# A gated convolution and four pools on one Trainium2 core: spread of 1/rms one group earlier, a PSUM bank for each pool product, evacuations moved up

## Reference, cut to what matters

```python
x = rms_norm(h, norm_final)                  # end of the first block
...
xn = rms_norm_2(h, norm_mix[layer])
proj = einsum('bsd,de->bse', xn, w_in_even)  # 1024 x 2048
a_b, a_c, a_v, z_b = four slices of 512 of proj
y_a = a_b * causal_dwconv3(a_c * a_v, conv_a)
# multiscale_pool: 4 groups of 128 channels, windows 2, 4, 8, 16
outs.append((csg - shifted) / count - z32[:, :, g])
mixed = einsum('bsgc,gcd->bsgd', pooled, w_pool) * pool_scale
h = h + einsum('bse,ed->bsd', concatenate([y_a, y_b]), w_out_even)
```

## Time and profile before

| | us |
|---|---|
| median of three runs | 1690.48 |
| profiled execution, its own time | 1688.79 |
| its span | 1687.6 |
| TensorE busy in the span | 1608.8 |
| VectorE busy | 906.3 |
| ScalarE busy | 680.5 |
| GpSimd busy | 81.7 |
| `even` and `oe`, from 1110.29 to 1207.02 of the span | 96.73 |

### The profile page before, as it was taken

One profiled execution on the slowest core, in us unless ns is written; L12 is line 12 of the kernel. 1 busy time (PEld: TensorE's weight loads), 2 busy tenths in 40 slices (PEclk: granted clock), 3 DMA queues, 4 the chain that ended last, 5 costly groups with the idle time before them and its releaser, 6 DMA issues.

```text
span 1687.6 us, 25828 instructions
## 1 busy us (share of the span) xinstructions
PE 1608.8 (95%) x11251; PEld 1412.5 (84%) x11251; DVE 906.3 (54%) x1199; ACT 680.5 (40%) x917; POOL 81.7 (5%) x124
## 2 busy tenths in 40 slices
PE   5899999989999999989898999987999999999998
PEld 3678866767777778878668999987999999899998
DVE  4522277463243333356766555547677755477763
ACT  2411266342221221235564444433455445354452
POOL 4000043000000000000000000005000000000000
PEclk7799999999999999999898999998999999899999
DMA  9754542335554542243103555545455464455552
GB/s 254 236 195 151 175 36 23 119 107 200 174 185 165 174 150 94 81 149 124 53 2 103 197 176 170 183 156 172 150 176 185 160 205 150 135 181 184 178 178 70
DMA packets 242977, 251.27 MB, mean 149 GB/s; under 512 B 4797, under 2 KB 240672, under 8 KB 242864
## 3 DMA queue, kind: packets, MB, share of 16 engines
q1 hardware_dynamic: 240112, 244.34, 44.5%
q0 software_dynamic: 2464, 5.09, 2.6%
q10 hardware_dynamic: 288, 0.19, 0.0%
HBM read 248.55 MB, written 1.05 MB: 148 GB/s over the span
## 4 chain that ended last, share of the span: by engine, by line
PE 91%; DVE 4%; DMA 2%; ACT 1%; issue 1%; SPq 0%; DVEq 0%; ACTq 0%
PE psum L318 88%; PE psum L732 2%; DMA raw<-in_ada_w 2%; DVE wl L302 1%; DVE sums L795 1%; DVE pt L809 1%; ACT wh L295 0%; DMA raw<-in_na_w_qkv 0%; DVE acc L957 0%; DVE acc L1406 0%; ACT scr L762 0%; DVE hT L965 0%; DVE proj L1690 0%; DVE xl L458 0%; DVE scr L448 0%
## 5 line engine op out<-in xcount | busy, mean ns | idle before, releaser
L318 PE MATMUL psum<-xh,wh 128*128 128x256 f32 (+1 forms) x1936 | 620.7, 321 | 8.3 <-DVE wl L302 4.9
L318 PE MATMUL psum<-xl,wh 128*128 128x256 f32 (+1 forms) x1936 | 613.4, 317 | 0.0
L318 PE MATMUL psum<-xh,wl 128*128 128x256 f32 (+1 forms) x1936 | 612.5, 316 | 0.0
L302 DVE TENSOR_TENSOR wl<-raw,wh 128x2048 fp32r<-128x2048 f32 (+1 forms) x186 | 418.2, 2250 | 316.8 <-ACT wh L295 316.6
L295 ACT ACTIVATE wh<-raw 128x2048 fp32r<-128x2048 f32 (+1 forms) x186 | 347.9, 1874 | 401.7 <-PE psum L318 396.1
L318 PEld LDWEIGHTS psum<-xh,wh 128*128 128x128 f32 x1936 | 374.8, 194 | 48.4 <-issue 13.9
L318 PEld LDWEIGHTS psum<-xh,wl 128*128 128x128 f32 x1936 | 374.4, 193 | 22.7
L318 PEld LDWEIGHTS psum<-xl,wh 128*128 128x128 f32 x1936 | 374.9, 194 | 21.3 <-issue 0.5
L318 PE MATMUL psum<-ah,wh 128*128 128x256 f32 (+1 forms) x704 | 218.6, 310 | 0.0
L318 PE MATMUL psum<-al,wh 128*128 128x256 f32 (+1 forms) x704 | 218.1, 310 | 0.0
L318 PE MATMUL psum<-ah,wl 128*128 128x256 f32 (+1 forms) x704 | 217.9, 310 | 0.0
(11 more groups left out here) (239 smaller groups left out, 1612.4 us busy)
## 6 DMA issues: line engine op xcount, KB each, us to landing
raw<-in_ada_w SPq DMA_DIRECT2D x48, 1024.0 KB, 5.1
raw<-in_ffn_w_in SPq DMA_DIRECT2D x44, 1024.0 KB, 5.0
raw<-in_w_ffn_gate SPq DMA_DIRECT2D x22, 1024.0 KB, 5.1
raw<-in_w_ffn_up SPq DMA_DIRECT2D x22, 1024.0 KB, 5.1
raw<-in_ffn_w_out SPq DMA_DIRECT2D x16, 1024.0 KB, 5.0
raw<-in_w_ffn_down SPq DMA_DIRECT2D x16, 1024.0 KB, 5.0
raw<-in_na_w_qkv SPq DMA_DIRECT2D x12, 1024.0 KB, 5.3
raw<-in_w_in_even SPq DMA_DIRECT2D x8, 1024.0 KB, 5.6
```

The lines of the kernel that those rows point to most:

```text
L302: dve.e.tensor_tensor(wl[:, c % NSPL, 0:z], raw[:, p % NRAW, 0:z], wh[:, c % NSPL, 0:z].bitcast(F32), ALU.subtract).then_inc(W.lo, 1)
L318: return pe.e.matmul(o, l, r, start=start, stop=stop, skip_group_check=shared)
```

## The change

The two copies into `rstd` become a function of their own, `double_copy_act`, which ScalarE calls in step 1, behind the high split of that step. The spread stands behind group 1. The four pool products get the banks 6, 7, 4 and 5; products 0 and 1 follow group 5, products 2 and 3 follow group 6; the wait for the copy of the product before is replaced by waits for the copies out of bank 7 and for the evictions of banks 4 and 5. On VectorE, `evac` 0 and 1 go to step 1, `evac(2)` and `conv_first(0)` to step 2, `evac(3)` and `conv_rest(0)` to step 3, the hT products one step up, the pool low parts ahead of `evac(6)` and `evac(7)`. On ScalarE the pool copies go ahead of the gate's. The first piece of `oe` waits for seven evictions instead of eight.

```diff
+        def double_copy_act():
             act.wait_ge(N.spread, 5)
             act.e.activation(rstd[:, 0:T], stat[:, T:TT], ACT.Copy).then_inc(N.copy, 1)
             act.e.activation(rstd[:, T:TT], stat[:, 0:T], ACT.Copy).then_inc(N.copy, 1)
...
-        OE = Down("oe", 1, bank[0:4], (mixh, mixl), lambda i: pe.wait_ge(E.evac, 8), None, lambda k: vcol(V_NFFN2 + k), (xh5, xl5), 5)
+        OE = Down("oe", 1, bank[0:4], (mixh, mixl), lambda i: pe.wait_ge(E.evac, 7 if i == 0 else 8), None, lambda k: vcol(V_NFFN2 + k), (xh5, xl5), 5)
+        pbank = (bank[6], bank[7], bank[4], bank[5])
...
         def pool_mm(x):
             pe.wait_ge(E.pooled, x + 1)
-            if x:
-                pe.wait_ge(E.scaled, x)
-            mm(bank[6][:, 0:T], wp[:, g, :], scr[:, x, 0:T], True, True).then_inc(E.turned, 1)
+            if x == 1:
+                pe.wait_ge(N.copy, 2)
+            elif x >= 2:
+                pe.wait_ge(E.evac, x + 3)
+            mm(pbank[x][:, 0:T], wp[:, g, :], scr[:, x, 0:T], True, True).then_inc(E.turned, 1)
...
                 if j == 0:
                     late_stat_pe(D1)
-                elif j == 2:
+                elif j == 1:
                     spread_pe(4, 4)
                 elif j == 5:
                     pool_mm(0)
+                    pool_mm(1)
                 elif j == 6:
-                    pool_mm(1)
-            pool_mm(2)
-            pool_mm(3)
+                    pool_mm(2)
+                    pool_mm(3)
...
-                act.e.activation(s, bank[6][:, 0:T], ACT.Copy, scale=vcol(V_PSC + POOLS[x])).then_inc(E.scaled, 1)
+                act.e.activation(s, pbank[x][:, 0:T], ACT.Copy, scale=vcol(V_PSC + POOLS[x])).then_inc(E.scaled, 1)
...
                 if j == 0:
                     double_act()
+                elif j == 1:
+                    double_copy_act()
                 elif j == 3:
                     conv_act(0)
                 elif j == 6:
                     conv_act(1)
+                    pool_act(0)
+                    pool_act(1)
+                elif j == 7:
                     gate_act(0)
-                    pool_act(0)
-                elif j == 7:
-                    gate_act(1)
-                    pool_act(1)
-            pool_act(2)
-            pool_act(3)
+                    pool_act(2)
+                    pool_act(3)
+            gate_act(1)
...
                 if j == 0:
                     double_dve()
-                elif j == 3:
+                elif j == 1:
                     evac(0)
                     evac(1)
+                elif j == 2:
                     evac(2)
+                    conv_first(0)
+                elif j == 3:
                     evac(3)
-                    conv_first(0)
+                    conv_rest(0)
                 elif j == 4:
-                    conv_rest(0)
                     evac(4)
                 elif j == 5:
                     evac(5)
                     conv_first(1)
                 elif j == 6:
                     conv_rest(1)
+                    pool_lo(0)
+                    pool_lo(1)
                     evac(6)
                     gate_lo(0)
                 elif j == 7:
+                    pool_lo(2)
+                    pool_lo(3)
                     evac(7)
-                    pool_lo(0)
                     gate_lo(1)
-                if j in (3, 4, 5, 6):
-                    for k in (2 * j - 6, 2 * j - 5):
+                if j in (2, 3, 4, 5):
+                    for k in (2 * j - 4, 2 * j - 3):
...
-            for x in (1, 2, 3):
-                pool_lo(x)
```

## The result

The changed kernel took 1667.17 us (median of 4 runs, 1665.4 to 1667.3) against 1690.82 us beside it: ratio 0.9859, 95% interval 0.9842 to 0.9876. That is 23.6 us less. The profiled execution took 1667.2 us, its span is 1665.9, 21.7 us under the span of before.

A forecast was written before the change was run, and what follows sets the result against it. TensorE bounds the kernel. Savings of 4.9, 2.3, 6.3 and 6.9 us, less a 2.1 us new wait and 0.8 for products, give 17.5 (17.6 by schedule): 1671.2 profiled, 1672.9 us median; range 1668.8 to 1679.5.

The forecast's parts named there:

- Bound and place: TensorE, busy 95% of the span, bounds; time is won only in its idle or slow-clock stretches from `even` to `oe`.
- Spread behind group 1: Spread needs no wait; before group 3, 4.87 us of idle and 2.29 us of lower clock go.
- Low splits hidden: VectorE's low splits, behind moved evacuations, still end before TensorE needs them; least margin 4.9 us.
- I cost this at nothing on the path: VectorE's evacuations moved up add no time on TensorE's path; GpSimd's chain then begins at about 1127.8.
- GpSimd's chain, the mis-sized term: Fourth pooled tile at 1158.6: 26.0 us plus 4.2 for two stops and 0.6; product 3 waits about 2.1 us.
- Clock after that wait: TensorE runs slow in group 7 after product 3's wait: 1.5 us taken, lower bound nothing.
- Group 1 stays: Group 0, the column sums and group 1 keep their profiled times on TensorE; group 1 ends at 1125.34.
- my 79.1 us: Forecast length of the stage from the first matmul of `even` to the end of `oe`, against 96.73 us profiled.
- rival 1: GpSimd is in time for product 3; TensorE waits 0.8 us before `oe`; 20.4 us less, 1670.1 us; chance 0.28.
- "The gain is kept whole" behind `oe`: Behind `oe`, splits and loads keep their distance to TensorE, so the 17.6 us gained in the stage stays whole.
- the median 1.7 above the profile: The median of runs lies 1.7 us above the profiled execution, turning the forecast 1671.2 us into 1672.9.
- The range: Low end 1668.8 us takes in GpSimd being in time; high end 1679.5 a fourth tile as late as about 1165.

The follow-up runs named there:

- three-addition run: Changed kernel with three more 128 x 256 additions on GpSimd ahead of its fourth tile, result not used; 1671.31 us, ratio 0.9882.
- the repeated after: The changed kernel measured once more, nothing edited; 1667.17 us, ratio 0.9863.
- the last kernel: Changed kernel with column sums inside group 1, product 3 behind group 7 and the first piece of `oe` reordered; 1665.62 us, ratio 0.9861.
- the kernel with hT products moved: Changed kernel with VectorE's eight products with hT moved behind the loop, out of GpSimd's time; 1671.79 us, ratio 0.9884.
- eight additions: Changed kernel with eight more 128 x 256 additions on GpSimd ahead of its fourth tile; 1675.87 us, ratio 0.991.

## Why the prediction was wrong, step by step

The mechanism was right, and so was the sign. What failed are terms of the sum, none of them larger than 2 us: the growth of GpSimd's chain (4.8 us assumed, 3.1 measured, and so a wait of 2.1 us that was 0.62), the slow clock of group 7 (1.5 us assumed, nothing measured), group 1's slow stretch (1.5 us carried over, nothing measured), and what lies outside the stage. In detail:

- *Bound and place.* Right. TensorE's idle times in the stage were the gain, and the three largest went.
- *Spread behind group 1.* Right: no stall before group 3, copies at 1126.86, and the spread without a wait. This part alone gave 6.6 us, with the wait before product 1 some 1.2 us longer.
- *Low splits hidden.* Right. Every low split was in time.
- *"I cost this at nothing on the path" (VectorE's moved evacuations).* True of the whole schedule, in which I had them start GpSimd at 1127.8. But this part carries 9.0 us of the gain once the others are in, which the text did not say.
- *GpSimd's chain, the mis-sized term.* I added 4.2 us for two more stops and 0.6 for other work to the 26.0 of before. It grew by 3.1 us in all. The five stops cost 9.4 us (the rows above less what such an operation takes unstopped, 0.2 to 0.6), the three of before 5.7: 3.7 more, since the operation at 1148.17 came when the low split (1147.34 to 1149.80) was a third over and was stopped for 1.4 us only. The rest cost 0.6 less than before, not 0.6 more. GpSimd's start and TensorE's arrival both came some 1.5 us sooner after the stage's first matmul than forecast, by group 1, so the chain decides: the wait before product 3 was 0.62 us instead of 2.1, 1.5 us less.
- *Clock after that wait.* I took 1.5 us "after 1.90 and 6.33 us of idle". The three-addition run shows just this price behind 2.80 us, the changed kernel none behind 0.62: another 1.5 us. It may have hung on the term before: no run has a wait of 2.1 us there. My low bound allowed for it.
- *Group 1 stays.* This step failed for a reason of its own: I carried the slow stretch of one trace (1.5 us) on as a fixed part, under "Group 0, sums and group 1 stay". It was there in 3 of the 11 traces that have the 0.91 us pause.
- These three terms make 4.5 us, all of the difference between my 79.1 us and the measured 74.6. `oe` also began without rival 1's 0.8 us of waiting for VectorE.
- *"The gain is kept whole" behind `oe`, and the median 1.7 above the profile.* Behind the stage 480.6 us were left in before and in six of the experiments, 479.1 in after, the repeated after and the last kernel, up to 483.5 in others, in steps of 1.5 us with slow stretches behind the same pauses. The stage itself began anywhere from 1109.3 to 1113.5 us. The changed kernel's median lies at its profiled execution, not 1.7 above; in its repeat it lies 2.9 above, so the 1.7 of one trace was chance too. The whole miss is 1672.9 - 1667.2 = 5.7 us: 4.5 in the stage, 1.5 behind it and 1.7 of that surcharge, less 2.0 by which the stage began late. So the measured gain of 23.6 us is partly luck; 21.3 to 22.1 of it are the stage's.
- *The range.* Its low end rested on rival 1, which kept group 1's slow stretch. Without it rival 1 gives 1668.6, and one step of 1.5 us elsewhere brings 1667.1. A low end that follows the rows would have let each slow stretch behind a short pause be there or not.

Open: why the steps outside the stage fall one way for some kernels in most of their executions (the kernel with hT products moved had 1670.2 to 1672.0 in four runs, the changed one 1664.3 to 1668.6 in eight) and where they fall in executions that were not profiled. The changed kernel and its repeat both have 479.1 us behind the stage. The runs with three and eight additions changed almost only the stage's length, and have 482.1 and 480.5: the steps moved with it, but not in proportion, and one trace each does not show a rule.

## What to carry to other kernels

When a step is freed by several edits, cost them in one schedule: here the parts alone gave 6.6 and 2.8 us and all together 21.3, since each wait hid the next. Work moved up on one engine is worth what it starts on another (GpSimd), even where its own engine had room. And do not carry one trace's slow stretch behind a short pause over as a fixed term: here, behind 0.91 us of idle and the sums, it was some 1.5 us in 3 of 11 traces and nothing in the others, so it belongs in the range.

## What the runs showed of the hardware

- The slow pitch (0.21 us a matmul, 1.2 GHz, against 0.12 at 2.4 GHz) after idle time of TensorE: none after 0.62 and 1.50 us; 1 and 15 matmuls in two kernels after the same 2.94 us; 15 or 16 after 2.80, 3.15 and 4.29; 22 to 26 after 4.87 behind the spread; 11 and 14 after 6.33 and 6.03, 11 after 5.96 and 14 after 7.22. In three traces 17 to 20 in `oe` followed 1.90 us, product 2, 0.66 us and product 3, so 1.90 us was not harmless there. Over these waits the length does not grow with the idle time. After 0.91 us of idle and 0.9 us of one-column sums it was 1 matmul in eight traces and 15 to 17 in three.
- VectorE and GpSimd hold each other up, in both directions. GpSimd's operation at 1135.34 took 2.67 us beside a low split that began at 1135.26; VectorE's product L1701, 0.42 us at best, took 0.98 beside a GpSimd addition that began 0.02 us sooner. From VectorE's timeline of the changed kernel:

```profile
1140.23 0.98 DVE L1701 TENSOR_TENSOR proj<-proj,rstd 128x256 f32<-128x256 f32 x1
```

and from GpSimd's:

```profile
1140.21 0.71 POOL L1623 TENSOR_TENSOR ptmp<-ptmp 128x248 f32<-128x248 f32 x1
```

- So the exclusive lock that the Trainium skill states (page "SBUF — State Buffer", section "Who interferes with whom") is what single pairs of rows look like. The sum over a chain is another matter: taking 8 VectorE operations of 0.44 us out of GpSimd's time shortened it by 0.9 us, not 3.5. That both engines pause between operations and short ones slip in is my reading of it; no run tests it.
